# Four dense networks: three block-product pairs each, with two weight sums per pair made by accumulating transfers from GpSimd

## The reference, cut to what matters

```python
def swiglu(x, w_gate, w_up, w_down):
    return (jax.nn.silu(x @ w_gate) * (x @ w_up)) @ w_down

# twice per layer, two layers
h = h + 0.5 * swiglu(rms_norm_2(h, ffn_norm[layer, 0]), ffn_w_gate[layer, 0], ...)
```

## Time and profile before

| what | value |
|---|---|
| median of three runs | 2225.48 us |
| the profiled execution, its own time | 2225.49 us |
| its span in the profile | 2223.6 us |
| PE busy over the span | 94% |
| DVE, ACT, POOL busy over the span | 54%, 36%, 1% |
| the four dense networks in the span | about 1213 to 1398, 1505 to 1690, 1690 to 1874, 2033 to 2209 us |

### The profile page before, as it was taken

One profiled execution on the slowest core, in us unless ns is written; L12 is line 12 of the kernel. 1 busy time (PEld: TensorE's weight loads), 2 busy tenths in 40 slices (PEclk: granted clock), 3 DMA queues, 4 the chain that ended last, 5 costly groups with the idle time before them and its releaser, 6 DMA issues.

```text
span 2223.6 us, 27395 instructions
## 1 busy us (share of the span) xinstructions
PE 2086.9 (94%) x10956; PEld 1279.9 (58%) x10956; DVE 1190.4 (54%) x1785; ACT 808.0 (36%) x1263; POOL 28.1 (1%) x38
## 2 busy tenths in 40 slices
PE   5999999999999899889976999999999999989998
PEld 3447743333333333323322888778888888867887
DVE  6976612222222222222214877677886886685976
ACT  6045321121111111101102555565555554375544
POOL 0000000000000000000000000100000000200000
PEclk8999989999999999999998999999999999999999
DMA  7782799999999999999999452327445443414451
GB/s 325 267 319 105 274 420 416 415 426 427 427 428 427 427 428 428 427 426 428 428 426 410 195 227 113 119 102 286 191 159 205 169 171 136 167 44 174 186 211 45
DMA packets 49845, 633.85 MB, mean 285 GB/s; under 512 B 5809, under 2 KB 5809, under 8 KB 6993
## 3 DMA queue, kind: packets, MB, share of 16 engines
q1 hardware_dynamic: 49712, 632.04, 69.3%
HBM read 630.97 MB, written 1.05 MB: 284 GB/s over the span
## 4 chain that ended last, share of the span: by engine, by line
PE 74%; DMA 16%; DVE 4%; ACT 4%; issue 1%; SPq 0%; DVEq 0%; ACTq 0%
DMA piece<-in_moe 16%; PE bank L2429 13%; PE bank L2306 13%; PE bank L2308 13%; PE bank L2307 13%; PE bank L2470 6%; PE bank L2404 3%; PE bank L2494 2%; PE bank L1059 2%; PE bank L2948 1%; PE bank L3018 1%; PE bank L746 1%; PE bank L372 1%; PE bank L2445 1%; DVE prob_n L1302 1%
## 5 line engine op out<-in xcount | busy, mean ns | idle before, releaser
L2429 PE MATMUL bank<-piece,xeT 128*64 128x512 f32 (+1 forms) x2304 | 445.0, 613 | 53.2 <-DMA piece<-in_moe 45.2
L2312 DVE TENSOR_TENSOR ffn_lo<-slot,ffn_hi 128x2048 fp32r<-128x2048 f32 x148 | 337.7, 2289 | 100.1 <-ACT ffn_hi L3272 99.6
L3272 ACT ACTIVATE ffn_hi<-slot 128x2048 fp32r<-128x2048 f32 x148 | 281.7, 1914 | 119.0 <-PE bank L2308 107.0
L2429 PEld LDWEIGHTS bank<-piece,xeT 128*64 128x64 f32 (+1 forms) x2304 | 134.1, 130 | 330.0 <-issue 305.6
L2550 DVE TENSOR_TENSOR hT<-hT,bank 128x512 f32<-128x512 f32 x144 | 92.2, 682 | 257.9 <-PE bank L2494 257.8
L2306 PE MATMUL bank<-ffn_hi,hT_hi 128*128 128x512 f32 x512 | 202.3, 395 | 0.0
L2308 PE MATMUL bank<-ffn_hi,hT_lo 128*128 128x512 f32 x512 | 199.7, 390 | 0.0
L2307 PE MATMUL bank<-ffn_lo,hT_hi 128*128 128x512 f32 x512 | 199.4, 389 | 0.0
L2599 DVE TENSOR_SCALAR work<-bank 128x256 f32<-128x256 f32 x60 | 25.5, 425 | 323.5 <-PE bank L2438 323.5
L2662 ACT ACTIVATE work<-bank 128x256 f32<-128x256 f32 x30 | 11.5, 384 | 289.6 <-PE bank L2445 289.6
L2308 PE MATMUL bank<-ffn_hi,act_lo 128*128 128x512 f32 x288 | 114.3, 397 | 0.0
(11 more groups left out here) (789 smaller groups left out, 3257.3 us busy)
## 6 DMA issues: line engine op xcount, KB each, us to landing
piece<-in_moe SPq DMA_DIRECT2D x190, 2048.0 KB, 25.9
slot<-in_ffn SPq DMA_DIRECT2D x44, 2048.0 KB, 8.1
slot<-in_ffn SPq DMA_DIRECT2D x44, 1024.0 KB, 7.9
slot<-in_ada SPq DMA_DIRECT2D x16, 1024.0 KB, 5.3
slot<-in_nsa_in SPq DMA_DIRECT2D x5, 2048.0 KB, 8.5
slot<-in_merge SPq DMA_DIRECT2D x3, 3072.0 KB, 12.8
slot<-in_ada SPq DMA_DIRECT2D x2, 3072.0 KB, 18.8
slot<-in_w_in SPq DMA_DIRECT2D x6, 1024.0 KB, 7.8
```

The costliest lines, as they stand in the source:

```text
L2312: return dve.tensor_tensor(lo, x, hi.bitcast(F32), ALU.subtract)
L2429: mm = pe.matmul(bank[n * c:n * (c + 1), :], x[:, kt, :], w[i][:, at:at + 512], start=kt == 0, stop=False)
L3272: act.activation(k["ffn_hi"][:, room, :], ffn_plain(k, q, what), ACT.Copy).then_inc(s["ffn_down_hi"] if isinstance(what, int) else s["ffn_ ...
```

## The change

1. Each network has three pairs, at steps 3 and 4, 6 and 7, 9 and 10 (`FFN_PAIRS`); plain are 0, 1, 2, 5 and 8. The network now ends with a pair, and the last two down products are 10 and then 9.
2. The signs of the block sums are turned so that all weight sums are additions: T1 = B11 + B12, T3 = B12 + B22, T2 = B22 + T1, T4 = T2 + B21. `rows_sums` and two joins use a two-operation form (`scalar_tensor_tensor`) for the turned signs.
3. T1 and T3 leave DVE. GpSimd issues three transfers of 1024 KB per pair (new function `ffn_pair_sums`): B12 is copied from memory into `behind`; then, once step m+1 has landed, B22 is added from memory onto B12 in the ring slot (T3, an accumulating transfer); then, once the copy has landed, B11 is added from memory onto `behind` (T1). For the second and third pair the copy waits until the form of the T1 before it is made. DVE's T2 now waits for T1's transfer, ACT's form of T3 for the other.
4. The loads on SP have another order (`FFN_LOADS`), the rooms of the down forms too.
5. The order on ACT and DVE at a network's start changes: the form of down 0 now stands ahead of piece 0 of step 1, and the row sums move ahead of `turned_low(0)`. In the middle pair the form of down m-1 stands behind the seventh block's.
6. Some semaphores are shared, and waits of the mixers' first forms follow the new order of the downs.

```diff
-FFN_PAIRS = (4, 8)
-FFN_DOWNS = (0, 1, 2, 3, 5, 4, 6, 7, 9, 8, 10)
+FFN_PAIRS = (3, 6, 9)
+FFN_DOWNS = (0, 1, 2, 4, 3, 5, 7, 6, 8, 10, 9)
...
-FFN_LOADS = [(what, m) for what, group in (("both", (0, 1, 2)), ("down", (0, 1, 2))) for m in group]
-for step in (3, 4, 5, 6):
-    FFN_LOADS += [("both", step), ("down", step)]
-FFN_LOADS += [(what, m) for what in ("both", "down") for m in (7, 8, 9)] + [("both", FFN_LAST), ("down", FFN_LAST)]
+FFN_LOADS = [(what, m) for what, group in (("both", (0, 1, 2)), ("down", (0, 1, 2)), ("both", (3, 4, 5)), ("down", (3, 4))) for m in group]
+FFN_LOADS += [("both", 6), ("both", 7), ("down", 5), ("down", 7), ("both", 8), ("down", 6), ("both", 9), ("both", 10), ("down", 8), ("down", 10), ("down", 9)]
...
-PAIR_SUMS = ("T1", "T3", "T2", "T4")
+PAIR_SUMS = ("T2", "T4")
...
-        if name == "T1":
-            ins = dve.tensor_tensor(t1, b12, b11, ALU.subtract)
-        elif name == "T3":
-            ins = dve.tensor_tensor(b12, b22, b12, ALU.subtract)
-        elif name == "T2":
-            dve.wait_ge(s["ffn_sum"], sum_count(q, m, "T1"))
+        if name == "T2":
+            dve.wait_ge(s["cross_sum"], 32 * pair_number(q, m) + 32)
             dve.wait_ge(s["ffn_w_lo"], FFN_COUNT * q + FFN_FORMS[m, "A11 B11"])
-            ins = dve.tensor_tensor(t2, b22, t1, ALU.subtract)
+            ins = dve.tensor_tensor(b11, b22, k["behind"][:, 0:PIECE], ALU.add)
...
+def ffn_pair_sums(k, pool, q):
+    s = k["sig"]
+    for m in FFN_PAIRS:
+        at = pair_number(q, m)
+        first, second = (k["plan"][f"ffn{q}_{n}"] for n in (m, m + 1))
+        rows = [k["src"]["ffn"][FFN_STEPS * q + n, :, :] for n in (m, m + 1)]
...
+        if m == FFN_PAIRS[0]:
+            pool.wait_ge(s["ffn_sum"], 10 * q + 4)
+        else:
+            pool.wait_ge(s["ffn_w_lo"], FFN_COUNT * q + FFN_FORMS[m - 3, "S1 T1"])
+            pool.wait_ge(s["ffn_sum"], sum_count(q, m - 3, "T2"))
+        cross = k["behind"][:, 0:PIECE]
+        pool.dma_start(cross, rows[1][:, 0:PIECE]).then_inc(s["cross_sum"], 16)
+        pool.wait_ge(k["landed"][second.slot], second.landed)
+        wide = ffn_slot(k, q, m + 1)[:, 0:PIECE]
+        pool.dma_start(wide, rows[1][:, PIECE:2 * PIECE], accum_op=ALU.add).then_inc(s["wide_sum"], 16)
+        pool.wait_ge(s["cross_sum"], 32 * at + 16)
+        pool.dma_start(cross, rows[0][:, 0:PIECE], accum_op=ALU.add).then_inc(s["cross_sum"], 16)
...
     i = FFN_NORM[q]
     ffn_norm_scalar(k, act, i, gain, 0)
     if q == 0:
         high(0, 1)
     ffn_norm_scalar(k, act, i, gain, 1)
+    high(0)
     high(1, 0)
```

More of the change, by code:

```diff
@@ L2760, in pair @@
     def pair(m):
-        spare = DOWN_ROOM[m + 1]
-        for n, room in enumerate((spare, 0, 1, spare, 0, 1, spare)):
+        for n, room in enumerate((3, 0, 1, 3, 0, 1, 3)):
             forms[m, FFN_BLOCKS[n]] = len(forms) + 1
@@ L2779, in ffn_turns @@
         down(m - 1)
-        plain(m + 2, 0)
+        if m + 2 < FFN_STEPS:
+            plain(m + 2, 0)
         down(m + 1)
-        plain(m + 2, 1)
+        if m + 2 < FFN_STEPS:
+            plain(m + 2, 1)
         down(m)
[L2784 to L2787, removed]
     return forms, turns
@@ L3171, in join @@
             dve.wait_ge(s["ffn_joined"], joined_count(q, m, "W"))
-            ins = dve.tensor_tensor(keep, keep, c, ALU.add)
+            ins = dve.scalar_tensor_tensor(out=keep, in0=keep, scalar=-1.0, in1=c, op0=ALU.mult, op1=ALU.subtract)
         elif name == "U3":
@@ L3176, in join, with first_sum, pair @@
             dve.wait_ge(s["ffn_joined"], joined_count(q, m, "U3"))
-            ins = dve.tensor_tensor(fourth, third, c, ALU.add)
+            ins = dve.scalar_tensor_tensor(out=fourth, in0=third, scalar=-1.0, in1=c, op0=ALU.mult, op1=ALU.subtract)
         else:
-            ins = dve.tensor_tensor(third, third, d, ALU.subtract)
+            ins = dve.tensor_tensor(third, third, d, ALU.add)
         ins.then_inc(s["ffn_joined"], 1)
-    def pair(m):
+    def first_sum(m):
+        pair_landed(m)
+    def pair(m, between=None):
+        last = m + 2 == FFN_STEPS
         low(m, "A11 B11")
-        pair_landed(m)
-        pair_sum(m, "T1")
-        turned_low(m - 2)
-        pair_sum(m, "T3")
+        if between is not None:
+            between()
+        pair_sum(m, "T2")
         low(m, "S4 B22")
-        pair_sum(m, "T2")
         swiglu(m - 1)
@@ L3192, in pair @@
         pair_sum(m, "T4")
-        low(m - 1)
+        if between is not None or last:
+            low(m - 1)
         low(m, "S2 T2")
@@ L3199, in pair @@
         low(m, "A22 T4")
+        if between is None and not last:
+            low(m - 1)
         for name in PAIR_JOINS[1:5]:
             join(m, name)
-        low(m + 2, 0)
+        if not last:
+            low(m + 2, 0)
         swiglu(m + 1)
@@ L3206, in pair @@
         low(m + 1)
-        turned_low(m + 1)
-        low(m + 2, 1)
-        low(m)
-        turned_low(m)
+        if last:
+            turned_low(m + 1)
+            low(m)
+        else:
+            turned_low(m + 1)
+            low(m + 2, 1)
+            turned_low(m)
+            low(m)
+            first_sum(m + 3)
     i = FFN_NORM[q]
@@ L3216, in ffn_vector @@
     ffn_norm_vector(k, dve, i, gain, 1)
+    low(0)
     low(1, 0)
@@ L3312, in keep, with pair @@
         act.activation(k["behind"][:, 2048 + 512 * n:2560 + 512 * n], pair_banks(k, q, m)[bank], ACT.Copy).then_inc(s["ffn_kept"], 1)
-    def pair(m):
+    def pair(m, between=None):
+        last = m + 2 == FFN_STEPS
         high(m, "A11 B11")
-        turned_high(m - 2)
+        if between is not None:
+            between()
         high(m, "S4 B22")
@@ L3319, in pair @@
         high(m, "A12 B21")
-        high(m - 1)
+        if between is not None or last:
+            high(m - 1)
         keep(m, 0)
@@ L3327, in pair @@
         high(m, "A22 T4")
-        high(m + 2, 0)
+        if between is None and not last:
+            high(m - 1)
+        if not last:
+            high(m + 2, 0)
+        else:
+            high(m + 1)
         silu(m + 1)
         silu(m)
-        high(m + 1)
+        if not last:
+            high(m + 1)
         turned_high(m + 1)
-        high(m + 2, 1)
-        high(m)
-        turned_high(m)
+        if last:
+            high(m)
+        else:
+            high(m + 2, 1)
+            turned_high(m)
+            high(m)
     i = FFN_NORM[q]
@@ L3346, in ffn_scalar @@
     silu(0)
[L3347 removed]
     turned_high(0)
     high(2, 0)
[L3350 removed]
+    sums_high()
     silu(1)
     high(2, 1)
[L3353 to L3365 removed]
+    high(1)
+    pair(FFN_PAIRS[0], lambda: turned_high(1))
+    for m in FFN_PAIRS[1:]:
+        pair(m)
     if q == 1:
         ffn_weights_high(k, act, 2, 0, 0)
[L3368 removed]
+    turned_high(FFN_DOWNS[-1])
     if q == 1:
@@ L4021, in cmp_weights_tensor @@
     s = k["sig"]
[L4022 removed]
+    pe.wait_ge(s["cmp_p"], 4)
     for half in range(2):
```

131 lines of the change are left out of this document (58 added, 73 removed).

## The result

| what | before | changed |
|---|---|---|
| median of the runs | 2225.62 us (2225.2 to 2227.72, 4 runs) | 2317.12 us (2313.57 to 2322.46, 4 runs) |
| ratio to before | | 1.0411, 95% interval 1.0389 to 1.0434 |
| the profiled execution, its own time; span | 2225.49; 2223.6 us | 2313.57; 2311.7 us |

The changed kernel is 4.1% slower. It was forecast slower, at 2247 us with a range of 2217 to 2276; the measured time lies outside that range, just above the 2263 to 2313 of the rival in which the sums are far slower than copies.

The account below looks back on a forecast made before the run. PE was taken to bound the dense networks. From 2225.5 us, less 10.9 for matmuls, plus 12.1 for starts, 2 for clock and 18 for late sums, came 2246.7, say 2247 us; range 2217 to 2276.

Parts of the forecast that it names:

- the rival in which the sums are far slower than copies: Ahead of pairs: each sum takes 12 us, one behind the other, T1 at E + 33; 2263 to 2313 us, chance 0.24.
- What bounds the kernel: In the dense networks PE alone sets the end; matmuls removed or waits added change the time one for one.
- 48 matmuls, -10.9 us: One more pair in each of four networks saves a block of 12 matmuls, 2.72 us each: -10.9 us.
- The start, +12.1 us: Starts of networks two and four: ACT waits for down 0's load, delaying step 1's forms; PE waits 6.4 and 5.7 us.
- The sums, +18 us: Ahead of pairs: T1 lands late, delaying T2; 1 us middle pair, 3.5 last, 0 first, times four networks: +18 us.
- half of the loads: Ahead of pairs: SP's loads, if all ahead of the sums, make T1 6 to 10 us later; half was taken.
- the 2 MB row: Ahead of pairs: lower price for both sums, two plain transfers together as one of 2 MB, 7.4 us.
- the deadline: DVE must begin T2 in time for a pair's fourth block: by E + 25.1 in the middle pair, E + 22.9 otherwise.
- some 12 us: Ahead of pairs: the amount the forecast would lack if GpSimd's sums did not share the 16 engines with SP's loads.
- The clock, +2 us: Behind long PE waits at the network starts: half clock for a few us, 0 to 3 us each, +2 us in all.
- The sums are hidden: Ahead of pairs: rival with sums at a plain copy's price, only the start costing; 2226.7 to 2229 us, chance 0.22.
- The faster case: Starts and pairs: rival with sums hidden and down 0 landed before ACT needs it; 2214.6 to 2221 us, chance 0.12.

Follow-up runs that it names:

- e2: Changed kernel with GpSimd's sum T1 issued ahead of the wait for step m+1 and of T3's sum: 2236.28 us, ratio 1.0048.
- e3: Changed kernel with T1's sum issued first and, in networks two and four, the form of down 0 back behind silu(0): 2223.53 us, ratio 0.9986.
- e9: As e3, with the rooms of the turned activations of steps 9 and 10 exchanged: 2218.47 us, ratio 0.9964.
- e4: Changed kernel with both accumulating transfers issued as plain copies, same order and waits, weight sums not formed: 2246.15 us, ratio 1.0089.
- e8: Changed kernel with the wait for step m+1 kept ahead of both sums, but T1's sum issued ahead of T3's: 2240.72 us, ratio 1.0062.
- e7: Changed kernel with 1 MB GpSimd copies and sums added at the fourth network's end, to time them without SP loads; profiled execution 2322.37 us.

## Why the prediction was right and wrong

**What bounds the kernel: right.** Where PE's waits went, the time went with them (e2, e3, e9).

**48 matmuls, -10.9 us: right.** The count is 48 lower; e9, with most waits taken away, is 8.2 us below the kernel before that ran beside it (2226.66 us), and has 1.9 us of waits for forms left. So some 8 of the 10.9 us are shown as a gain.

**The start, +12.1 us: right in place and size.** 5.66 and 6.46 us, in networks two and four alone, behind ACT's wait for down 0, as worked out from the earlier trace rows. That the sum of 12.1 agrees to 0.1 us is luck in part, as 6.4 and 5.7 were forecast. e3 against e2 puts it at 12.8 us. What the sum could not say is that it would be worth 5.3 us as long as the other loss stood.

**The sums, +18 us: the mechanism right, the term mis-sized.** PE's waits for these forms are 47.0 + 4.1 = 51.1 us. The step that failed is T1's landing: "both then as two of 2 MB together, 13.0 us", and half of the loads, some 16.5 us from T3's issue in all. In the first network it took 22.8 us in the middle pair (1298.97 to 1321.78) and 18.5 in the last. The price of one sum was about right: 7.9 us alone, 7.4 for the 2 MB row. What was too low is what two of them take among the loads: two 2 MB loads landed 4.2 us apart, T1 6.8 to 8.0 us behind T3, and the company of the loads was taken at half: T3 took 15.3 us in the middle pair, beside a 1 MB load issued 2.5 us before it and a 2 MB load 0.8 us behind. How the excess divides between the second sum and the loads stays open, since no run has two sums in flight without loads. T1 landed at E + 32.9 there (E, the end of the seventh block, is 1288.84), against the forecast E + 26. In the last pair it was E + 27.6 (1373.46; E 1345.83), against E + 26.4, about right. P, the next pair's first matmul, came at E + 28.3, as forecast from the earlier trace rows, and the waits fit the deadline: in the last pair 1.08 at the second block and 3.57 at the fourth. Per network the forecast was 1 us in the middle pair and 3.5 in the last; they had 5.2 to 6.4 and 4.3 to 5.9.

The Trainium skill, "Collectives: The Full Stack", "The bandwidth ceiling: the fold count and why AG ≠ RS ≠ AR", has a reducing transfer of a four-rank ring at half the rate of a copy. In the time that a transfer holds the DMA engines the trace nearly agrees, about 1.9 times (the estimate under e4); in the time to landing it is 7.9 to 5.1 us for 1 MB, 1.55 times.

The prediction's "some 12 us" that the sum would lack if the loads did not share does not follow from its own figures: T1 at E + 22.5 is ahead of both times wanted, so all 18 would go.

Two smaller misses in the same term: first pairs were put at 0, and had 4.5, 0, 2.9 and 1.0 us; and the deadline was taken from the fourth block alone, where in the middle pair the second block was the first to wait, its form being behind T2 on DVE. The prediction had named that form as held, without a price.

**The clock, +2 us: wrong.** PE's products ran 32.3 us slower. This term failed by nearly as much as the sums did. The earlier trace rows showed the lower clock after 4.2 us without work; the term took one short stretch of it for two waits. There were 16 waits of PE at forms besides, and 12 of them were followed by one, as was each start wait: 0.65 of full clock over 7.6 us behind the wait of 6.4. So a wait of 6 us costs some 8 to 9 in all.

**The network's new end, not in the sum: 4.5 us.** Four waits of 1.13 us for `act_lo` stood in the changed kernel and in every run up to e8, and went with e9. The prediction had no term for a network that ends with a pair. Of the 70 us between the forecast and the measured time, some 33 are the sums, 30 the clock and 4.5 this end.

**The rivals.** "The sums are hidden" was wrong by the add: e4, with copies, is at 2246, and even there the T2 wait is 19.6 us. The faster case needed both waits away, which e9 then did by order and an exchange of two rooms: 2218 us, inside its 2215 to 2221. "Far slower" was nearest, and had T1 at E + 33, which is where it landed in the first network's middle pair. But its 84 us were all PE's waits for sums of 12 us each; measured were 51 us of these waits and 32 of clock, at 7.9 us for a sum alone, so that the total came near is partly luck.

## What to carry to other kernels

When work is moved from an engine to transfers in one in-order queue, write down for each transfer when its result is wanted, and issue by that: the first wanted stood last here, and moving three lines was worth 81 us of 91. Price a kind of transfer by rows that show it among its neighbours; if there are none, measure one first, alone and in its place. Undo suspected losses together as well as singly: one of two in a chain, taken away alone, showed 5 us of its 13. And a long wait of a dense TensorE has a second price in clock.

## What the runs showed of the hardware

- An accumulating transfer of 1 MB took 7.9 us alone, where a copy from the same queue took 5.1 (e7). It held the 16 DMA engines about 1.9 times as long as a copy, 5.3 against 2.8 us, an estimate from the queue's shares in the changed kernel and e4.
- Such a transfer beside two loads of 2 MB took 15.5 us (e3), and the second load 17.7 us in place of the changed kernel's 13.1.
- After 6.4 us with next to no matmul the granted clock was 0.65 over the next 7.6 us, and 1.00 over the 11 us behind these; behind waits of about 1 us it stayed at 1.00.
